# Head norm factor of 14 heads through memory instead of through TensorE

## The chip, the cores and the metric

One Trainium2 chip, one of its cores. The metric is the device time of one execution in microseconds (us). TensorE (PE in the profile) multiplies matrices, VectorE (DVE), ScalarE (ACT) and GpSimd (POOL) do the work on elements, SyncE (SP) issues DMAs, and 16 DMA engines move the data. Each engine runs its instructions in the order in which they are written and waits on semaphores for the others.

## The reference

A trunk of two layers over 512 positions of width 1024, in float32. Each layer is a half-step SwiGLU, a mixer and a second half-step SwiGLU. The mixer projects the normed input to q, k, v, an output gate, a convolution's input and two gates, runs a gated delta rule over 8 heads of width 128 and a depthwise convolution of 31 taps, and mixes the two. The part that matters here is the norm of each head's output:

```
def rmsnorm(x, w):
    xf = x.astype(jnp.float32)
    y = xf * lax.rsqrt(jnp.mean(xf * xf, axis=-1, keepdims=True) + EPS)
    return (y * w.astype(jnp.float32)).astype(x.dtype)

    o = gated_delta_chunked(q, k, v, g, beta)
    o = rmsnorm(o, head_norm) * jax.nn.silu(g_out.reshape(shp).astype(jnp.float32))
    y_a = o.reshape(bsz, seq, KEY_WIDTH).astype(h.dtype) @ w_a_out
```

The head's output stands with its 128 channels in the partitions and the 512 positions along the free axis. The factor (the power -0.5 of the mean square) is one number for each position, so it has to be the same in all partitions before it can be multiplied on.

## The kernel before

Every large product is done in float32r in three passes: a weight tile is split into a rounded part w_hi (ScalarE) and a rest w_lo, the activations likewise, and TensorE adds hi*hi, hi*lo and lo*hi (function three). In the head stage the rest of the weights is made by ScalarE writing -w_hi into w_lo and GpSimd adding the raw weights to it by an accumulating DMA (function lo on GpSimd). SP loads the raw tiles into four slots.

For each layer the heads run as a pipeline. While TensorE runs the delta rule of head rn it also runs the projections of head rn+1, six tiles t = 0 to 5 of 12 pieces each. The list PE_ORDER sets how they alternate: H is one such piece, two 512-column matmuls; the other names are steps of the delta rule. The delta rule inverts a triangular matrix by doubling in six levels lv = 0 to 5, each of which is xt{lv}, y{lv} and xy{lv} on TensorE. ScalarE makes the pieces XO{lv}, XE{lv} of X for xt{lv} and y{lv}. VectorE makes YD (L1623) out of y{lv}'s result, and xy{lv} waits for YD and XT. Behind each YD VectorE does what the tuple behind[lv] says: "t" is a tap of the long convolution (about one 512-column instruction, cacc), (0, j), (1, j), (2, j) are taps of the short convolutions of q, k and v, "oF", "ohi", "olo" belong to the tail.

The tail of head rn-1 (the norm of its output) runs within head rn. ScalarE squares the output, GpSimd adds a term ("sum"), TensorE sums over the partitions by four matmuls with a column of ones ("so"), VectorE adds a constant (vE), GpSimd takes the power -0.5 ("rs", function mean_root, L1896), which leaves 128 x 4 numbers in sm. TensorE then turns the four columns, each spread over 128 columns, into bank 5 ("fb", L725), VectorE multiplies (oF, L1715) and splits the product into o_hi and o_lo (L1718, L1721), which TensorE reads only after the last head. The tail of head 7 of each layer runs after the heads with the same steps.

GpSimd's order in a head is: sum, the product for qd, rs, the second power rk, then the accumulating DMAs of the tiles c0+3, c0+4, ..., c0+8, each as soon as ScalarE has written the negative (L861). hf0 is the buffer hf[0]: ScalarE copies the convolution's value tile there (valb, L1012) at t = 4, and VectorE reads it as craw (L1567) in level 0 of the next head.

Of the kernel before, what the change touches and what calls it, by code (L numbers as in the profile page):

```python
# [17 lines left out]
P = 128  # L18
# [69 lines left out]
PE_ORDER = "H H gr kt H kk kq H so H H H x2t vt H H H xt0 y0 H H fb xy0".split()  # L88
# [8 lines left out]
PE_STEPS = [x for x in PE_ORDER if x not in ("H", "so", "fb")]  # L97
PE_TAIL = ["so", "fb"]
# [18 lines left out]
def trunk(nc, x, params_in, ffn1_w_gate, ffn1_w_up, ffn1_w_down, w_in, w_ab, a_log, dt_bias, head_norm, w_a_out, w_b_out, w_o,  # L117
          ffn2_w_gate, ffn2_w_up, ffn2_w_down, consts, out):
    ds = bass.ds
    with ExitStack() as ctx:  # L120
# [63 lines left out]
        valb, gth, sgn, sgc, og = hf[0], hf[1], sqb[0], sqb[1], ssq  # L184
        S, R, VN = (sb(n, [P]) for n in ("S", "R", "VN"))
# [33 lines left out]

        def sem(name):  # L220
            return ctx.enter_context(nc.semaphore(name))
# [24 lines left out]
        ghi_done = sem("ghi_done")  # L246
        mrinv_done = sem("mrinv_done")
# [188 lines left out]
        def _(pe):  # L436
# [138 lines left out]
            for l in range(DEPTH):  # L575
# [139 lines left out]
                def tail(name, rn):  # L715

                    if name == "so":
                        pe.wait_ge(po_tl.sem, po_tl.after(rn, "sum"))
                        pe.wait_ge(ve_tl.sem, ve_tl.after(rn - 1, "oF"))
                        for c in range(NC):  # L720
                            m = mm(bank[5][:, c:c + 1], attn[:, c * P:c * P + P], ones[:, 0:1])
                    else:
                        pe.wait_ge(po_tl.sem, po_tl.after(rn, "rs"))
                        for c in range(NC):
                            m = nc.tensor.transpose(bank[5][:, c * P:c * P + P], whole(sm[:, 5, c:c + 1]), ident)  # L725
                    m.then_inc(*pe_tl.step(name))

# [64 lines left out]
                for m_ in range(PRE):  # L792
                    c = 2 * PRE + m_
                    first_unit(c)
                    for k in range(KT - 1):
# [10 lines left out]
                        if m_ == 1 and k == 4:  # L806
                            tail("fb", last)
# [42 lines left out]
        def _(act):  # L850
# [112 lines left out]
            for l in range(DEPTH):  # L963
# [17 lines left out]
                def dense_steps(t, Rd, c0, rd):  # L981
# [28 lines left out]
                    elif t == 4:  # L1010
                        act.wait_ge(ve_cr.sem, ve_cr.after(rd - 1, "craw"))
                        nc.scalar.activation(valb[:, :], bk[:, :], ACT.Copy).then_inc(*ac_ds.step("val"))  # L1012
# [216 lines left out]
        def _(dve):  # L1229
# [164 lines left out]
            for l in range(DEPTH):  # L1394
# [124 lines left out]
                def head(dense, hn, rn, before=True):  # L1519
# [75 lines left out]
                    behind = [("l", "a", "l", "c"), ("oF", "t", "ohi", "t", "olo", "t"), ((0, 0), "t", (0, 1), "t", (0, 2)),  # L1595
                              ("t", "t", "t", "t", "t"), ((1, 0), "t", (1, 1), "t", (1, 2)),
# [108 lines left out]
                def tail(name, rn, hn=None):  # L1705
# [7 lines left out]
                    elif name == "oF":  # L1713
                        dve.wait_ge(pe_tl.sem, pe_tl.after(rn, "fb"))
# [247 lines left out]
```

## Time and profile before

| | us |
|---|---|
| median of 3 runs | 2720.67 |
| lowest and highest | 2720.61, 2720.92 |
| the profiled execution | 2720.52 |
| its span, first to last instruction | 2718.7 |

Mean granted TensorE clock 0.999. Busy shares of the span: TensorE 100%, VectorE 58%, ScalarE 40%, GpSimd 9%. The time of an execution holds 1.8 us around the span. In a timeline row the first number is the start and the second the duration; matmuls and also neighbouring instructions of one engine overlap by a little, so the distance between starts, not the duration, is what one costs. A bracket at the end says how long the engine was idle before it and what ended that. Where rows of several kinds of matmul are merged, line 438 is the helper through which most of them are issued.

### The profile page before, as it was taken

Reading aid. Unit: us, or ns where it says so; the run is one execution under the profiler, and the core shown is the slowest. Engines: PE = TensorE matmul, PEld = TensorE weight load, DVE = VectorE, ACT = ScalarE, POOL = GpSimd, SP = SyncE. Lnnn points to the kernel's source line nnn. Section 1 sums busy time; section 2 is a strip of 40 time slices with the busy share of each in tenths; the row PEclk is TensorE's granted clock in tenths of the full one; section 3 lists DMA queues with packets and bytes.
Section 4 is the critical chain, followed back from the end, with each engine's and each line's share of the span. In section 5 each row is a group of like instructions: output and inputs, shape, how many; then the busy total and the mean of one; then the engine's idle time right before and its main releaser. Section 6 shows DMA issues by size and latency. Waiting matters only on the chain.

```text
span 2718.7 us, 35832 instructions
## 1 busy us (share of the span) xinstructions
PE 2705.3 (100%) x13096; PEld 2251.9 (83%) x13096; DVE 1581.7 (58%) x2504; ACT 1100.1 (40%) x1849; POOL 258.2 (9%) x231
## 2 busy tenths in 40 slices
PE   9999999999999999999999999999999999999998
PEld 7888878888887888888888888788888878888887
DVE  6554357888885345553355543688888943455532
ACT  4222247766663232222222222566676622322222
POOL 0000022122120010000000000211212100100000
PEclk9999999999999999999999999999999999999999
DMA  4223335554542222233322233455556332222332
GB/s 166 96 97 104 92 101 140 130 142 111 136 126 93 98 88 100 93 101 93 102 93 93 100 93 96 108 131 140 125 124 145 96 108 93 93 100 93 97 94 66
DMA packets 84603, 292.04 MB, mean 107 GB/s; under 512 B 10001, under 2 KB 12689, under 8 KB 84497
## 3 DMA queue, kind: packets, MB, share of 16 engines
q1 hardware_dynamic: 69232, 235.85, 26.5%
q0 software_dynamic: 14976, 54.53, 10.9%
q8 instruction: 64, 1.05, 0.2%
q14 instruction: 43, 0.34, 0.0%
q10 hardware_dynamic: 288, 0.27, 0.0%
HBM read 233.99 MB, written 2.10 MB: 87 GB/s over the span
## 4 chain that ended last, share of the span: by engine, by line
PE 97%; DVE 2%; ACT 0%; issue 0%; DMA 0%; DVEq 0%; POOLq 0%; POOL 0%; ACTq 0%
PE bank L438 95%; PE bank L637 1%; PE bank L689 1%; DVE c_lo L1747 0%; DVE w_lo L1235 0%; ACT c_hi L1191 0%; PE bank L651 0%; PE bank L725 0%; DVE sqb L1743 0%; DVE hf L1743 0%; DMA pcol<-in_params_in 0%; DVE hf L1738 0%; PE bank L458 0%; DVE NT L1664 0%; ACT w_hi L855 0%
## 5 line engine op out<-in xcount | busy, mean ns | idle before, releaser
L1235 DVE TENSOR_TENSOR w_lo<-raw,w_hi 128x1024 fp32r<-128x1024 f32 x342 | 422.6, 1237 | 542.2 <-ACT w_hi L855 542.1
L855 ACT ACTIVATE w_hi<-raw 128x1024 fp32r<-128x1024 f32 x446 | 469.8, 1055 | 658.7 <-PE bank L438 658.6
L438 PE MATMUL bank<-h_hi,w_hi 128*128 128x512 f32 x1504 | 587.1, 390 | 2.2 <-DVE h_lo L1260 2.1
L438 PE MATMUL bank<-h_hi,w_lo 128*128 128x512 f32 x1504 | 585.5, 389 | 0.0
L438 PE MATMUL bank<-h_lo,w_hi 128*128 128x512 f32 x1504 | 585.3, 389 | 0.0
L438 PE MATMUL bank<-g_hi,w_hi 128*128 128x512 f32 x928 | 384.2, 414 | 0.0
L438 PE MATMUL bank<-g_hi,w_lo 128*128 128x512 f32 x928 | 378.7, 408 | 0.0
L438 PE MATMUL bank<-g_lo,w_hi 128*128 128x512 f32 x928 | 369.6, 398 | 0.0
L438 PEld LDWEIGHTS bank<-h_hi,w_hi 128*128 128x128 f32 x1504 | 282.3, 188 | 63.3 <-issue 3.6
L438 PEld LDWEIGHTS bank<-h_hi,w_lo 128*128 128x128 f32 x1504 | 282.3, 188 | 58.8
L1535 DVE SCALAR_TENSOR_TENSOR cacc<-c_raw,ncol,cacc 128x512 f32<-128x512 f32 x464 | 330.0, 744 | 0.4
L438 PEld LDWEIGHTS bank<-h_lo,w_hi 128*128 128x128 f32 x1504 | 282.4, 188 | 57.7
L438 PE MATMUL bank<-act_hi,w_hi 128*128 128x512 f32 (+1 forms) x726 | 281.3, 387 | 0.0
L438 PE MATMUL bank<-act_hi,w_lo 128*128 128x512 f32 (+1 forms) x726 | 279.6, 385 | 0.0
L438 PE MATMUL bank<-act_lo,w_hi 128*128 128x512 f32 (+1 forms) x726 | 277.0, 382 | 0.0
L890 ACT ACTIVATE hf<-hf 128x512 f32<-128x512 f32 x88 | 55.6, 632 | 447.3 <-DVE hf L1282 447.3
L1845 POOL TENSOR_TENSOR ssq<-ssq,sqb 128x512 f32<-128x512 f32 x41 | 54.8, 1337 | 1708.0 <-ACT sqb L869 1708.0
L438 PEld LDWEIGHTS bank<-g_hi,w_lo 128*128 128x128 f32 x928 | 175.0, 189 | 31.3
L438 PEld LDWEIGHTS bank<-g_lo,w_hi 128*128 128x128 f32 x928 | 175.5, 189 | 28.2
L438 PEld LDWEIGHTS bank<-g_hi,w_hi 128*128 128x128 f32 x928 | 175.9, 190 | 22.9
L438 PEld LDWEIGHTS bank<-act_hi,w_lo 128*128 128x128 f32 x726 | 136.2, 188 | 30.0
L438 PEld LDWEIGHTS bank<-act_lo,w_hi 128*128 128x128 f32 x726 | 136.3, 188 | 28.7
(258 smaller groups left out, 3355.5 us busy)
## 6 DMA issues: line engine op xcount, KB each, us to landing
raw<-in_w_in SPq DMA_DIRECT2D x128, 512.0 KB, 3.3
w_lo<-raw POOLq DMA_DIRECT2D x104, 512.0 KB, 4.6
raw<-in_ffn_w_gate SPq DMA_DIRECT2D x88, 512.0 KB, 3.2
raw<-in_ffn_w_up SPq DMA_DIRECT2D x88, 512.0 KB, 3.2
raw<-in_ffn_w_down SPq DMA_DIRECT2D x64, 512.0 KB, 3.5
raw<-in_ffn_w_down SPq DMA_DIRECT2D x32, 384.0 KB, 3.1
raw<-in_w_a_out SPq DMA_DIRECT2D x16, 512.0 KB, 3.2
raw<-in_w_b_out SPq DMA_DIRECT2D x16, 512.0 KB, 3.2
```

The source lines that it names most:

```text
L438: return nc.tensor.matmul(o, a, b, start=start, stop=stop, **kw)
L637: m = nc.tensor.transpose(o[:, c * P:c * P + P], a[:, c * P:c * P + P], ident)
L689: m = nc.tensor.transpose(bank[2][:, q * P:q * P + P], X[:, q * P:q * P + P], ident)
L855: nc.scalar.activation(w_hi[c % SLOTS][:, :], raw[c % SLOTS][:, :], ACT.Copy).then_inc(hi_done, 1)
L890: nc.scalar.activation(sg_f[f][:, :], sg_f[f][:, :], ACT.Silu).then_inc(silu_done, 1)
L1235: tt(w_lo[c % SLOTS][:, :], raw[c % SLOTS][:, :], w_hi[c % SLOTS][:, :].bitcast(F32), ALU.subtract).then_inc(lo_v, 1)
L1535: stt(out=acc[:, :], in0=src, scalar=ncol[:, j:j + 1], in1=acc[:, :], op0=ALU.mult, op1=ALU.add).then_inc(taps, 1)
L1845: tt(ssq[:, :], ssq[:, :], sqb[m % 2][:, :], ALU.add).then_inc(sums, 1)
```

## The change

For the heads 0 to 6 of each layer (14 in all) the factor no longer goes through TensorE. GpSimd, right after the power, writes the 128 x 4 numbers to a scratch in memory (rs_rows, one row of 512 for each head, 4-byte pieces), and later in the same head, behind the weight DMA of tile c0+4, reads that row into all 128 partitions (factor_row), into hf[0], between its use as craw and its next use as valb. VectorE's oF, ohi and olo stand behind YD of level 3 instead of level 1 and the five taps of level 3 stand in level 1; oF waits for the row and multiplies by it out of SBUF. ScalarE's valb waits for the oF of two heads before. In PE_ORDER "fb" is gone and xt0 y0 stand one H earlier. The last head's tail keeps its four columns (last_factor_spread).

```
--- before.py
+++ after.py
@@ -85,7 +85,7 @@
 
 
 
-PE_ORDER = "H H gr kt H kk kq H so H H H x2t vt H H H xt0 y0 H H fb xy0".split()
+PE_ORDER = "H H gr kt H kk kq H so H H H x2t vt H H xt0 y0 H H H xy0".split()
 for _l in range(1, LEVELS):
     PE_ORDER += ("H H H " if _l < LEVELS - 1 else "H H H H ").split() + f"xt{_l} y{_l} H H H xy{_l}".split()
 PE_ORDER += "H H H xtf H H H vn0 H H os0".split()
@@ -94,8 +94,8 @@
 HALVES = 12
 LATE = 8
 assert PE_ORDER.count("H") == 6 * HALVES, PE_ORDER.count("H")
-PE_STEPS = [x for x in PE_ORDER if x not in ("H", "so", "fb")]
-PE_TAIL = ["so", "fb"]
+PE_STEPS = [x for x in PE_ORDER if x not in ("H", "so")]
+PE_TAIL = ["so"]
 
 DVE_STEPS = ["hs", "kT", "qT", "dmin", "skE", "rden", "bnk2", "neg", "NT", "x2T", "vT", "yd0", "attnT"]
 DVE_STEPS += [f"yd{_l}" for _l in range(1, LEVELS)]
@@ -182,6 +182,7 @@
             sb(n, [SEQ]) for n in "qT kT dec thv attn qd NT X XT Y".split())
 
         valb, gth, sgn, sgc, og = hf[0], hf[1], sqb[0], sqb[1], ssq
+        row = hf[0]
         S, R, VN = (sb(n, [P]) for n in ("S", "R", "VN"))
         hsc = sb("hsc", [HEADS, HS_N, NC])
         hs = sb("hs", [HS_N, NC])
@@ -216,6 +217,8 @@
         csum, csq = hf[1], (hf[0], sqb[0])
 
         bank = [ctx.enter_context(nc.psum_tensor(f"bank{i}", [P, SEQ], F32)) for i in range(8)]
+
+        rs_rows = nc.dram_tensor("rs_rows", (DEPTH * HEADS, SEQ), F32, kind="Internal").ap()
 
         def sem(name):
             return ctx.enter_context(nc.semaphore(name))
@@ -244,6 +247,9 @@
         hf_done = sem("hf_done")
         hhi_done = sem("hhi_done")
         ghi_done = sem("ghi_done")
+        fb_done = sem("fb_done")
+        rs_out = sem("rs_out")
+        row_in = sem("row_in")
         mrinv_done = sem("mrinv_done")
         scaled = sem("scaled")
         hlo_g = sem("hlo_g")
@@ -714,16 +720,19 @@
 
                 def tail(name, rn):
 
-                    if name == "so":
-                        pe.wait_ge(po_tl.sem, po_tl.after(rn, "sum"))
+                    pe.wait_ge(po_tl.sem, po_tl.after(rn, "sum"))
+                    if rn == l * 8 and l:
                         pe.wait_ge(ve_tl.sem, ve_tl.after(rn - 1, "oF"))
-                        for c in range(NC):
-                            m = mm(bank[5][:, c:c + 1], attn[:, c * P:c * P + P], ones[:, 0:1])
-                    else:
-                        pe.wait_ge(po_tl.sem, po_tl.after(rn, "rs"))
-                        for c in range(NC):
-                            m = nc.tensor.transpose(bank[5][:, c * P:c * P + P], whole(sm[:, 5, c:c + 1]), ident)
+                    for c in range(NC):
+                        m = mm(bank[5][:, c:c + 1], attn[:, c * P:c * P + P], ones[:, 0:1])
                     m.then_inc(*pe_tl.step(name))
+
+                def last_factor_spread(rn):
+
+                    pe.wait_ge(po_tl.sem, po_tl.after(rn, "rs"))
+                    for c in range(NC):
+                        m = nc.tensor.transpose(bank[5][:, c * P:c * P + P], whole(sm[:, 5, c:c + 1]), ident)
+                    m.then_inc(fb_done, 1)
 
                 def xy(lv, rn):
                     pe.wait_ge(ac_dn.sem, ac_dn.after(rn, f"XT{lv}"))
@@ -804,7 +813,7 @@
                             pe.wait_ge(var_done, l * 4 + 3)
                             tail("so", last)
                         if m_ == 1 and k == 4:
-                            tail("fb", last)
+                            last_factor_spread(last)
                         three(m_, c % SLOTS, k, o_hi, o_lo, k, k == 0, False)
                 for m_ in range(PRE):
                     if m_ == 0:
@@ -1009,6 +1018,8 @@
                         nc.scalar.activation(gth[:, :], bk[:, :], ACT.Tanh, scale=0.5).then_inc(*ac_ds.step("g_th"))
                     elif t == 4:
                         act.wait_ge(ve_cr.sem, ve_cr.after(rd - 1, "craw"))
+                        if rd >= l * 8 + 2:
+                            act.wait_ge(ve_tl.sem, ve_tl.after(rd - 2, "oF"))
                         nc.scalar.activation(valb[:, :], bk[:, :], ACT.Copy).then_inc(*ac_ds.step("val"))
                     else:
                         act.wait_ge(ve_sg.sem, ve_sg.after(rd, "sg"))
@@ -1019,6 +1030,8 @@
                     act.wait_ge(taps, l * (8 * CONV) + (m + 2) * CONV)
                     if m >= 3:
                         act.wait_ge(csq_done, l * 7 + (m - 2))
+                    elif m == 2:
+                        act.wait_ge(ve_tl.sem, ve_tl.after(l * 8 + 6, "oF"))
                     dst = csum if m == 0 else csq[m % 2]
                     nc.scalar.activation(dst[:, :], c_all[:, m, :], ACT.Square).then_inc(cf_done, 1)
 
@@ -1592,8 +1605,8 @@
                             return
                         gate_product(dense[0])
 
-                    behind = [("l", "a", "l", "c"), ("oF", "t", "ohi", "t", "olo", "t"), ((0, 0), "t", (0, 1), "t", (0, 2)),
-                              ("t", "t", "t", "t", "t"), ((1, 0), "t", (1, 1), "t", (1, 2)),
+                    behind = [("l", "a", "l", "c"), ("t", "t", "t", "t", "t"), ((0, 0), "t", (0, 1), "t", (0, 2)),
+                              ("oF", "t", "ohi", "t", "olo", "t"), ((1, 0), "t", (1, 1), "t", (1, 2)),
                               ("t", "t", (2, 0), "t", (2, 1), "t", (2, 2))]
 
                     def put(items):
@@ -1711,8 +1724,12 @@
                         dve.wait_ge(pe_tl.sem, pe_tl.after(rn, "so"))
                         a = ts(sm[:, 4, :], bank[5][:, 0:NC], P * EPS * EPS, None, ALU.add)
                     elif name == "oF":
-                        dve.wait_ge(pe_tl.sem, pe_tl.after(rn, "fb"))
-                        a = tt(og[:, :], og[:, :], bank[5][:, :], ALU.mult)
+                        if rn == l * 8 + 7:
+                            dve.wait_ge(fb_done, l + 1)
+                            a = tt(og[:, :], og[:, :], bank[5][:, :], ALU.mult)
+                        else:
+                            dve.wait_ge(row_in, (rn + 1 - l) * 16)
+                            a = tt(og[:, :], og[:, :], row[:, :], ALU.mult)
                     elif name == "ohi":
                         dve.wait_ge(ve_tl.sem, ve_tl.after(rn, "oF"))
                         a = ts(o_hi[:, hn, :], og[:, :], 1.0, None, ALU.mult)
@@ -1883,6 +1900,15 @@
                             h_rest(l, 4 * t)
                             h_rest(l, 4 * t + 2)
                         lo(Rd, G, c0 + t + 4)
+                        if t == 0 and rn is not None and before:
+                            factor_row(rn - 1)
+
+                def factor_row(rn):
+
+                    pool.wait_ge(rs_out, (rn + 1 - l) * 16)
+                    pool.wait_ge(ve_cr.sem, ve_cr.after(rn + 1, "craw"))
+                    src = rs_rows[rn].rearrange("(o s) -> o s", o=1)
+                    pool.dma_start(out=row[:, :], in_=src.broadcast_to([P, SEQ])).then_inc(row_in, 16)
 
                 def square_sum(rn):
 
@@ -1894,6 +1920,9 @@
 
                     pool.wait_ge(ve_tl.sem, ve_tl.after(rn, "vE"))
                     tt(sm[:, 5, :], sm[:, 4, :], pw[:, 0, :], ALU.pow).then_inc(*po_tl.step("rs"))
+                    if rn != l * 8 + 7:
+                        pool.wait_ge(po_tl.sem, po_tl.after(rn, "rs"))
+                        pool.dma_start(out=rs_rows[rn].rearrange("(c i) -> i c", c=NC), in_=sm[:, 5, :], allow_slow_non_contiguous=True).then_inc(rs_out, 16)
 
                 Gh = l * G_LAYER - 1
                 head(Rh, Gh, 0, None)
```

On VectorE, the piece of one head from the YD of level 3 to the YD of level 4. Before:

```order
L1623 TENSOR_TENSOR YD<-bank,cst 128x256
L1535 SCALAR_TENSOR_TENSOR cacc_95<-c_raw,ncol,cacc_95 128x512
L1535 SCALAR_TENSOR_TENSOR cacc_94<-c_raw,ncol,cacc_94 128x512
L1535 SCALAR_TENSOR_TENSOR cacc_95<-c_raw,ncol,cacc_95 128x512
L1535 SCALAR_TENSOR_TENSOR cacc_94<-c_raw,ncol,cacc_94 128x512
L1535 SCALAR_TENSOR_TENSOR cacc_95<-c_raw,ncol,cacc_95 128x512
L1623 TENSOR_TENSOR YD<-bank,cst 128x256
```

Now:

```order
L1636 TENSOR_TENSOR YD<-bank,cst 128x256
L1732 TENSOR_TENSOR ssq<-ssq,hf_74 128x512
L1548 SCALAR_TENSOR_TENSOR cacc_95<-c_raw,ncol,cacc_95 128x512
L1735 TENSOR_SCALAR o_hi<-ssq 128x512
L1548 SCALAR_TENSOR_TENSOR cacc_94<-c_raw,ncol,cacc_94 128x512
L1738 TENSOR_TENSOR o_lo<-ssq,o_hi 128x512
L1548 SCALAR_TENSOR_TENSOR cacc_95<-c_raw,ncol,cacc_95 128x512
L1636 TENSOR_TENSOR YD<-bank,cst 128x256
```

Lines 1732, 1735 and 1738 are oF, ohi and olo; hf_74 is hf[0], the row. They stood behind the YD of level 1 with three taps between them, and stand now behind the YD of level 3, with all that VectorE does later behind them.

On GpSimd, one head from the product for qd to the weights of tile c0+5. Before:

```order
L1876 TENSOR_TENSOR qd<-qd,qT 128x512
L1896 TENSOR_TENSOR sm<-sm,pw 128x4
L1879 TENSOR_TENSOR sm<-sm,pw 128x4
L1837 DMA w_lo_65<-raw_57 128x1024
L1837 DMA w_lo_62<-raw_54 128x1024
L1837 DMA w_lo_63<-raw_55 128x1024
```

Now:

```order
L1893 TENSOR_TENSOR qd<-qd,qT 128x512
L1922 TENSOR_TENSOR sm<-sm,pw 128x4
L1925 DMA rs_rows<-sm 128x4x1
L1896 TENSOR_TENSOR sm<-sm,pw 128x4
L1854 DMA w_lo_65<-raw_57 128x1024
L1854 DMA w_lo_62<-raw_54 128x1024
L1911 DMA hf_74<-rs_rows 128x512
L1854 DMA w_lo_63<-raw_55 128x1024
```

Two DMAs have come in: the write to the scratch ahead of the second power, and the read of the row between the weights of c0+4 and those of c0+5.

On TensorE, level 0 of one head from the turned X of level 0 to xy0. Before:

```order
L438 MATMUL bank<-g_lo,w_hi_58 128x512
L689 MATMUL bank<-cst,X 128x128 x2
L438 MATMUL bank<-X,Y 128x128 x2
L438 MATMUL bank<-g_hi,w_lo_62 128x512
L438 MATMUL bank<-g_hi,w_hi_58 128x512
L438 MATMUL bank<-g_lo,w_hi_58 128x512
L438 MATMUL bank<-g_hi,w_lo_62 128x512
L725 MATMUL bank<-cst,sm 128x128 x4
L438 MATMUL bank<-YD,XT 128x64x2 x2
```

Now (one row earlier, the last piece ahead of level 0 is not the same one):

```order
L444 MATMUL bank<-g_hi,w_lo_62 128x512
L695 MATMUL bank<-cst,X 128x128 x2
L444 MATMUL bank<-X,Y 128x128 x2
L444 MATMUL bank<-g_hi,w_hi_58 128x512
L444 MATMUL bank<-g_lo,w_hi_58 128x512
L444 MATMUL bank<-g_hi,w_lo_62 128x512
L444 MATMUL bank<-g_hi,w_hi_58 128x512
L444 MATMUL bank<-g_lo,w_hi_58 128x512
L444 MATMUL bank<-g_hi,w_lo_62 128x512
L444 MATMUL bank<-YD,XT 128x64x2 x2
```

L725 was the four turned columns, and the matmuls of X (L689, now L695) with those of X,Y are xt0 and y0. The columns are gone and one H, two rows of g, has moved from ahead of xt0 to behind y0.

## Rows read from the trace of the kernel before

**Rows 1.** The page: busy time by engine; the chain that ended last, by engine.

```profile
PE 2705.3 (100%) x13096; PEld 2251.9 (83%) x13096; DVE 1581.7 (58%) x2504; ACT 1100.1 (40%) x1849; POOL 258.2 (9%) x231
...
PE 97%; DVE 2%; ACT 0%; issue 0%; DMA 0%; DVEq 0%; POOLq 0%; POOL 0%; ACTq 0%
```

**Rows 2.** TensorE's waits: line, releaser, us in total, times, longest.

```profile
PE bank L438 <- DVE h_lo L1260: 2.1, 2, 1.9
```

**Rows 3.** Timeline of TensorE in one head: start us, us, instruction.

```profile
518.90 0.38 PE L689 MATMUL bank<-cst,X 128*128 128x128 f32 x2
...
520.49 0.60 PE L725 MATMUL bank<-cst,sm 128*128 128x128 f32 x4
520.92 0.61 PE L438 MATMUL bank<-YD,XT 128*128 128x128 f32 x4
521.29 0.48 PE L438 MATMUL bank<-g_hi,w_hi 128*128 128x512 f32 x1
```

**Rows 4.** The instructions of line 725: count, ns, first and last start.

```profile
L725 PE MATMUL bank<-cst,sm x64: 270/272/273, 471.4 to 2164.1; 128*128 128x128 f32 x64
```

**Rows 5.** Timeline of GpSimd in the same head.

```profile
517.66 1.52 POOL L1879 TENSOR_TENSOR sm<-sm,pw 128x4 f32<-128x4 f32 x1
519.47 0.92 POOL L1837 DMA_DIRECT2D w_lo<-raw  x1 [0.28 <-issue]
530.23 0.86 POOL L1837 DMA_DIRECT2D w_lo<-raw  x1 [9.85 <-ACT w_lo L861]
```

**Rows 6.** Timeline of ScalarE in the same head.

```profile
517.55 0.38 ACT L1079 ACTIVATE X<-bank 128x256 f32<-128x256 f32 x1
...
528.61 1.05 ACT L861 ACTIVATE w_lo<-raw 128x1024 fp32r<-128x1024 f32 x1
...
544.73 1.05 ACT L855 ACTIVATE w_hi<-raw 128x1024 fp32r<-128x1024 f32 x1
```

**Rows 7.** DMA from 530 to 535 us: busy tenths in 40 slices; issue and landing.

```profile
DMA  0000000000000986919919199097891990100000
...
w_lo<-raw POOLq DMA_DIRECT2D x1, 512.0 KB, 4.5
```

**Rows 8.** Timeline of VectorE in the same head.

```profile
523.97 0.68 DVE L1715 TENSOR_TENSOR ssq<-ssq,bank 128x512 f32<-128x512 f32 x1
524.56 0.54 DVE L1530 TENSOR_SCALAR cacc<-c_raw,ncol 128x512 f32<-128x512 f32 x1
...
525.35 0.48 DVE L1532 TENSOR_SCALAR cacc<-c_raw,ncol 128x512 f32<-128x512 f32 x1
...
526.35 0.75 DVE L1535 SCALAR_TENSOR_TENSOR cacc<-c_raw,ncol,cacc 128x512 f32<-128x512 f32 x1
...
531.41 0.42 DVE L1623 TENSOR_TENSOR YD<-bank,cst 128x256 f32<-128x256 f32 x1 [0.16 <-PE bank L438]
531.75 3.39 DVE L1535 SCALAR_TENSOR_TENSOR cacc<-c_raw,ncol,cacc 128x512 f32<-128x512 f32 x5
535.30 0.42 DVE L1623 TENSOR_TENSOR YD<-bank,cst 128x256 f32<-128x256 f32 x1 [0.16 <-PE bank L438]
...
538.30 0.74 DVE L1434 SCALAR_TENSOR_TENSOR ka<-k_raw,dcol,ka 128x512 f32<-128x512 f32 x1
```

**Rows 9.** Timeline of TensorE in the same head, later.

```profile
536.50 0.61 PE L438 MATMUL bank<-YD,XT 128*128 128x128 f32 x4
...
540.84 0.61 PE L438 MATMUL bank<-YD,XT 128*128 128x128 f32 x4
```

**Rows 10.** DMA at the end of the run: GB/s in 40 slices.

```profile
GB/s 344 353 297 315 372 344 344 344 358 334 353 348 226 5 0 0 0 0 0 0 0 80 358 339 301 358 358 334 344 320 372 353 330 348 367 245 14 0 0 0
```

**Rows 11.** DMA from 371 to 376 us: issues, KB each, us to landing.

```profile
wab_raw<-in_w_ab SPq DMA_DIRECT2D x1, 64.0 KB, 1.7
alb<-in_a_log SPq DMA_DIRECT2D x1, 4.0 KB, 2.8
```

**Rows 12.** Window at the end: busy by engine, granted clock, DMA share, GB/s.

```profile
2712.00:2718.00 6.00, 0.43 (x2) 0.19 (x2) 2.41 (x3) 0.00 (x0) 0.24 (x1) 0.68 0.65 218
```

More of the change, by code:

```diff
@@ L82, in after @@
         return (rnd + 1) * len(self.names) + self.at[name]
-PE_ORDER = "H H gr kt H kk kq H so H H H x2t vt H H H xt0 y0 H H fb xy0".split()
+PE_ORDER = "H H gr kt H kk kq H so H H H x2t vt H H xt0 y0 H H H xy0".split()
 for _l in range(1, LEVELS):
@@ L96 @@
 assert PE_ORDER.count("H") == 6 * HALVES, PE_ORDER.count("H")
-PE_STEPS = [x for x in PE_ORDER if x not in ("H", "so", "fb")]
-PE_TAIL = ["so", "fb"]
+PE_STEPS = [x for x in PE_ORDER if x not in ("H", "so")]
+PE_TAIL = ["so"]
 DVE_STEPS = ["hs", "kT", "qT", "dmin", "skE", "rden", "bnk2", "neg", "NT", "x2T", "vT", "yd0", "attnT"]
@@ L184, in trunk @@
         valb, gth, sgn, sgc, og = hf[0], hf[1], sqb[0], sqb[1], ssq
+        row = hf[0]
         S, R, VN = (sb(n, [P]) for n in ("S", "R", "VN"))
@@ L246, in trunk @@
         ghi_done = sem("ghi_done")
+        fb_done = sem("fb_done")
+        rs_out = sem("rs_out")
+        row_in = sem("row_in")
         mrinv_done = sem("mrinv_done")
@@ L715, in tail, with last_factor_spread @@
                 def tail(name, rn):
-                    if name == "so":
-                        pe.wait_ge(po_tl.sem, po_tl.after(rn, "sum"))
+                    pe.wait_ge(po_tl.sem, po_tl.after(rn, "sum"))
+                    if rn == l * 8 and l:
                         pe.wait_ge(ve_tl.sem, ve_tl.after(rn - 1, "oF"))
[L720 to L725, printed above, removed]
-                    m.then_inc(*pe_tl.step(name))
+                    for c in range(NC):
+                        m = mm(bank[5][:, c:c + 1], attn[:, c * P:c * P + P], ones[:, 0:1])
+                    m.then_inc(*pe_tl.step(name))
+                def last_factor_spread(rn):
+                    pe.wait_ge(po_tl.sem, po_tl.after(rn, "rs"))
+                    for c in range(NC):
+                        m = nc.tensor.transpose(bank[5][:, c * P:c * P + P], whole(sm[:, 5, c:c + 1]), ident)
+                    m.then_inc(fb_done, 1)
                 def xy(lv, rn):
@@ L1885, in head, with factor_row @@
                         lo(Rd, G, c0 + t + 4)
+                        if t == 0 and rn is not None and before:
+                            factor_row(rn - 1)
+                def factor_row(rn):
+                    pool.wait_ge(rs_out, (rn + 1 - l) * 16)
+                    pool.wait_ge(ve_cr.sem, ve_cr.after(rn + 1, "craw"))
+                    src = rs_rows[rn].rearrange("(o s) -> o s", o=1)
+                    pool.dma_start(out=row[:, :], in_=src.broadcast_to([P, SEQ])).then_inc(row_in, 16)
                 def square_sum(rn):
```

22 lines of the change are left out of this document (17 added, 5 removed).

## The prediction

> **What bounds the kernel now.** I read first the page: TensorE is busy in 2705.3 of 2718.7 us, and 97% of the chain that ended last is TensorE's own work [rows 1]. Then the waits of TensorE: the longest sum for one releaser is 2.1 us in the whole run [rows 2]. So TensorE never waits in the head stage. An instruction taken off it is worth its full time, and every microsecond for which a semaphore holds it is lost at once, as it runs in written order with nothing idle to take up the delay. What matters is therefore not VectorE's or GpSimd's busy share but how near each of their results comes to the TensorE instruction that wants it. For that I took the timelines of one head of layer 0 (the one whose four turned columns start at 520.49) and laid the engines beside each other. Heads follow each other every 49.12 us (the same columns start at 471.4 in the head before, the first start of [rows 4]), so one stands for the 14.
>
> **What is removed.** Four transposes of a column, L725, 64 in all [rows 4]: 16 groups, of which 14 go and the two of the last head of each layer stay. From the start of the group to the start of the next one, 520.49 to 520.92, it takes 0.43 us [rows 3], not the 0.60 shown as its duration, since matmuls overlap. 14 x 0.43 = 6.0 us saved. The place of xt0 and y0 moves forward by one H (two matmuls, some 0.47 us), so that three H stand between y0 and xy0 in place of two and the four columns. xt0 was at 518.90 and comes to 518.43; ScalarE's XE0, the later of the two pieces it needs, is over at 517.93 [rows 3, 6], so this makes no wait. Within the head everything TensorE does after them is then 0.43 us earlier, and ScalarE, which follows it, too.
>
> **What is added.** (1) GpSimd sends the 512 factors to memory, as 4-byte pieces. The pow that makes them is over when the next one starts, at 517.66, and GpSimd's next issue is at 519.47 [rows 5]. Its weight DMA keeps GpSimd 0.86 us for 128 pieces; four times the pieces cost between 0.86 and 3.4 us. Then the weight DMA of 519.47 starts at 520.4 to 523 and GpSimd is free by 524. After 519.47 it does nothing until 530.23, so I price this at nothing. SP's load into that slot waits for the weights' landing and comes as much later; ScalarE copies the slot next at 544.73 [rows 6], over ten microseconds on. Without that cover (beyond some 9 us) the DMA at 530.23 would be late.
> (2) GpSimd reads the row into 128 partitions, behind the weight DMA of 530.23 in its own order. That one waits for ScalarE's negative copy, 528.61 to 529.66 [rows 6]; 0.43 us earlier it starts at 529.80 and leaves GpSimd at 530.66. With the 0.28 us that GpSimd needs between its instructions [rows 5] the row's DMA starts at 530.94. Behind it is the next weight DMA, over five us later, so GpSimd itself has room.
> (3) VectorE's multiplication oF, ohi and olo move from level 1 to level 3, and oF waits for the row to land. Level 3 begins for VectorE with YD at 531.41 [rows 8], now 530.98, so VectorE asks for the row at 531.32: less than half a microsecond after its DMA is issued. That oF reads the row from SBUF and not from PSUM I price at nothing (one tensor_tensor of the same size, 0.68 us). ScalarE writes the row's buffer again as valb, behind its copy of 544.73, and waits there for an oF that is long over by then. Behind oF on VectorE are the rest of level 3 and then the YD of level 4, and for that YD waits TensorE's xy4 (the group at 536.50 [rows 9]).
>
> **When the row lands.** The trace shows no DMA queued right behind another of GpSimd's. It shows the one ahead of it alone: issued at 530.23, data in the slices from 531.6 to 534.4 on all engines, landed after 4.5 us [rows 7], some 0.4 us behind its last data. In the new run its data end 0.43 us earlier, at 533.9. The row's packets go to the same 16 engines from the same queue, so I let them start then. 0.26 MB at the 350 GB/s of a busy stretch [rows 10] take 0.75 us. Against that, the 4 KB of a_log read into 128 partitions took 2.8 us from issue, and 64 KB without repetition 1.7 [rows 11]: reading one place 128 times costs up to 1.1 us more, 1.85 in all. I take 1.1 us, nearer to the plain rate as the sum of bytes is large. Landing: 533.9 + 1.1 + 0.4 = 535.4; bounds with queueing 535.0 and 536.2.
> On the order of the packets the Trainium skill (DMA: Bandwidth & Descriptors, section Queues, rings and completion order) says that an engine works through the descriptors of one queue in the order in which they were put there. No row here shows it; by it the row stands behind the weights, as I take it.
>
> **From the row to TensorE.** oF and its companions with three taps between them: level 1 of before did it from 523.97 to 527.10 where the first two taps are short (0.54 and 0.48 us) [rows 8]. Level 3 has full taps of 0.74 us, so 3.13 + 0.20 + 0.26 = 3.59, less 0.08 us by which neighbours overlap (five taps of 0.74 take 3.39): 3.51 us to YD. YD 0.42 us, and 0.05 us each for the two semaphores, assumed: 4.03 us. xy4 can start at 535.4 + 4.03 = 539.43. Without a wait it would stand at 536.50 - 0.43 = 536.07. TensorE waits 3.36 us in each head.
> Is more lost behind it? Level 4 gives VectorE 3.74 us of work from YD to YD (535.30 to 539.04), so the next YD starts at 542.7 and ends at 543.1; xy5 stands 4.34 us behind xy4 [rows 9], at 543.8. No second wait. Nor is anything regained: all of TensorE's work behind xy4 waits with it.
> Sum: 14 x 3.36 = 47.0, less 6.0 = +41.0 us. The profiled execution took 2720.5 us (span 2718.7), within 0.2 us of the median shown, 2720.7. 2720.5 + 41.0 = 2761.5 us.
>
> **Rivals.**
> *The row is not held by the weights ahead of it* (15%). Landing then by GpSimd's own delay: issue at 530.94, 1.4 us to the first data [rows 7], 0.75 for the data and 0.4 to the landing: 533.5. xy4 at 537.53, a wait of 1.46, and 14 x (1.46 - 0.43) = 14.4: 2735 us. For it: slices with 1 or 0 stand between the full ones in [rows 7]. Against: the weight packets still have to be moved by the same engines.
> The Trainium skill (DMA: Bandwidth & Descriptors, section Anatomy of one DMA) prices a DMA of GpSimd at 2.0 us and its bytes at 436 GB/s: an estimate of 2.6 us for this one, which is the time of this rival. For the weights it gives 3.2 us where the trace has 4.5, so it is low for the DMA that decides here.
> *Reading one row 128 times is slow* (15%). The 1.1 us of a_log may come once for each 512 bytes, so four times here: landing at 533.9 + 4.4 + 0.4 = 538.7, xy4 at 542.73, a wait of 6.66, 14 x (6.66 - 0.43) = 87: 2808 us, and anything between 2775 and this. Only the two small rows of [rows 11] speak for it.
> *TensorE loses its clock in the wait* (7%). Its mean granted clock over the run is 0.999 (the full one, 2.4 GHz); it falls only after TensorE's last work, and the mean in 2712 to 2718 is 0.68 [rows 12]. A wait of 3.4 us is longer than any of before. If the 3.9 us of a level then ran at 1.2 GHz, twice as long, up to 14 x 3.9 = 55 us would come on top: 2816 us.
> *No wait at all, faster* (4%). The removed 6.0 us remain where the row lands by 532.0 (536.07 - 4.03): 2714.5 us. That is 1.1 us from its issue. The quickest DMA of these rows took 1.7 us and GpSimd's own 4.5. It decides only if the factor row's DMA gets ahead of the weight DMA, or the records of issue are late by more than a microsecond. A landing near 532.5 would make no difference that can be told (1%).
> *The row isn't what oF waits for*: were the write of the factors slow (over 9 us), its landing would hold the read and all of GpSimd's weights. That is a longer wait in the same place, and is in the upper part of the range.
>
> **How the numbers follow.** The forecast, a landing between 534.9 and 536.2, has 58% and alone gives 2755 to 2773. The range goes down to the unqueued row (2732), and up into the slow row's cases, to 2790: left out are 5% below and about half of the slow row and the clock's case above. What this measurement can tell from no change is 0.2%, 5.4 us. Slower by more than that: all cases but two, 0.94; within it 0.02; faster 0.04.
>
> **What would show it.** In the profile after: L725's successor has 8 instructions in place of 64. TensorE gets a row of waits, on its matmuls, for VectorE's YD, 14 times and 3.4 us each, about 47 us in all. VectorE is idle before the oF line for some 4 us each, put down to the row's DMA. The row's DMA has a time to landing near 4.5 us (2.6 with the rival). The heads come 52 us apart instead of 49.1. The prediction is wrong if oF does not wait (landing within a microsecond), if the DMA lands before the weights' ahead of it, or if the granted clock falls in the stage.

## The result, and the profile of the changed kernel

The changed kernel takes 2797.70 us (median of 4 runs, 2796.44 to 2798.78), the kernel before 2720.73 (4 runs, 2720.61 to 2720.92): ratio 1.0282, 95% interval 1.0268 to 1.0297. That is 77 us slower where 41 were forecast, and above the range, which ended at 2790. In the profiled executions the span went from 2718.7 to 2797.0 us: +78.3.

The page of after, busy time by engine and the chain by engine, against [rows 1]:

```profile
PE 2726.0 (97%) x13040; PEld 2263.9 (81%) x13040; DVE 1581.5 (57%) x2504; ACT 1101.9 (39%) x1849; POOL 272.5 (10%) x259
...
PE 89%; DVE 4%; DMA 3%; ACT 2%; issue 1%; POOL 0%; DVEq 0%; POOLq 0%; ACTq 0%
```

TensorE has 56 matmuls fewer and is busy 20.7 us longer. The chain, which was nearly all TensorE's own work, now runs in part through DMA and VectorE. The mean granted clock is 0.989, where it was 0.999. The two things to explain are thus a wait, and work that takes longer.

TensorE's waits in after, against [rows 2], and below them the first of VectorE's that is new:

```profile
PE bank L444 <- DVE YD L1636: 58.5, 14, 4.9
```

```profile
DVE ssq L1732 <- DMA hf<-rs_rows: 69.2, 14, 5.6
```

This is the wait forecast, at the place forecast, 14 times: oF (L1732) waits for the row, YD (L1636) stands behind oF, and xy4 behind YD. But it is 4.18 us a head, not 3.36. One head shows both parts. TensorE from the last matmul ahead of xy4 on, against [rows 9]:

```profile
543.28 0.39 PE L444 MATMUL bank<-g_lo,w_hi 128*128 128x512 f32 x1
543.51 0.39 PE L444 MATMUL bank<-g_hi,w_lo 128*128 128x512 f32 x1
548.78 1.20 PE L444 MATMUL bank<-YD,XT 128*128 128x128 f32 x4 [4.88 <-DVE YD L1636]
...
550.20 0.63 PE L444 MATMUL bank<-g_lo,w_hi 128*128 128x512 f32 x1
550.63 0.63 PE L444 MATMUL bank<-g_hi,w_lo 128*128 128x512 f32 x1
```

A 512-column matmul is 0.23 us from start to start ahead of the wait and 0.43 behind it. The windows of after show the granted clock (the column behind the engines'):

```profile
543.00:546.00 3.00, 0.90 (x4) 0.38 (x3) 1.32 (x3) 1.46 (x5) 0.87 (x1) 0.99 0.45 128
546.00:548.00 2.00, 0.00 (x0) 0.00 (x0) 2.00 (x5) 0.00 (x0) 0.00 (x0) 0.50 0.91 242
548.00:552.00 4.00, 3.22 (x10) 2.77 (x11) 3.94 (x7) 0.66 (x2) 0.00 (x0) 0.50 0.53 105
552.00:556.00 4.00, 4.00 (x23) 3.37 (x22) 2.15 (x4) 2.60 (x5) 0.00 (x0) 0.91 0.38 128
```

0.50 is the lower level, 1.2 GHz. It came within the wait of 4.88 us, at 545.9, when TensorE had stood still for 2.0 us; in other heads it came up to 1.2 us behind the wait's end. The clock fell in 12 of the 14 heads: 58.0 us at half clock in the head stages, in 47.6 of which TensorE worked. That work takes twice as long, so half of it is lost, 23.8 us.

Why the row is late is in the same head. GpSimd and, below, the DMAs issued there (KB, us to landing), against [rows 5, 7]:

```profile
525.65 0.85 POOL L1925 DMA_DIRECT2D rs_rows<-sm  x1 [0.30 <-POOL sm L1922]
526.52 1.05 POOL L1896 TENSOR_TENSOR sm<-sm,pw 128x4 f32<-128x4 f32 x1
527.51 0.95 POOL L1854 DMA_DIRECT2D w_lo<-raw  x1
537.48 0.86 POOL L1854 DMA_DIRECT2D w_lo<-raw  x1 [9.01 <-ACT w_lo L870]
538.02 0.90 POOL L1911 DMA_DIRECT2D hf<-rs_rows  x1
```

```profile
rs_rows<-sm POOLq DMA_DIRECT2D x1, 2.0 KB, 9.1
...
w_lo<-raw POOLq DMA_DIRECT2D x1, 512.0 KB, 9.7
...
w_lo<-raw POOLq DMA_DIRECT2D x1, 512.0 KB, 6.6
hf<-rs_rows POOLq DMA_DIRECT2D x1, 256.0 KB, 6.6
```

The write of the factors lands after 9.1 us. The weights of c0+3 behind it land after 9.7, at 537.2; SP, which waits for that to load the slot again, does so only then:

```profile
537.34 7.20 SPq L365 DMA_DIRECT2D raw<-in_w_in  x2
```

(Two loads merged: the first goes out at 537.34, the second at 544.21.) The first is in flight until 541.24, together with the weights of c0+4, issued at 537.48. These land after 6.6 us, and the row behind them after 6.6. VectorE, against [rows 8]:

```profile
538.65 0.42 DVE L1636 TENSOR_TENSOR YD<-bank,cst 128x256 f32<-128x256 f32 x1 [0.16 <-PE bank L444]
544.68 0.69 DVE L1732 TENSOR_TENSOR ssq<-ssq,hf 128x512 f32<-128x512 f32 x1 [5.61 <-DMA hf<-rs_rows]
...
548.22 0.42 DVE L1636 TENSOR_TENSOR YD<-bank,cst 128x256 f32<-128x256 f32 x1
```

oF starts at 544.68 and xy4 at 548.78: 4.10 us, forecast 4.03. The rest of the late time is the DMA's.

### The profile page after: what moved, and what is told of

It reads as the page before. It is cut to its first block, busy times and chain, and to the rows that moved or that the text cites. A ratio compares the mean times of both kernels' runs of the same rounds, so it can differ in the third digit from the quotient of the medians.

```text
span 2797.0 us, 35751 instructions
## 1 busy us (share of the span) xinstructions
PE 2726.0 (97%) x13040; PEld 2263.9 (81%) x13040; DVE 1581.5 (57%) x2504; ACT 1101.9 (39%) x1849; POOL 272.5 (10%) x259
## 4 chain that ended last, share of the span: by engine, by line
PE 89%; DVE 4%; DMA 3%; ACT 2%; issue 1%; POOL 0%; DVEq 0%; POOLq 0%; ACTq 0%
PE bank L444 88%; DMA hf<-rs_rows 3%; DVE cacc L1548 1%; PE bank L643 1%; PE bank L695 1%; ACT w_hi L864 1%; ACT w_lo L870 1%; DVE w_lo L1248 0%; DVE o_lo L1738 0%; DVE c_lo L1764 0%; DVE ssq L1732 0%; ACT c_hi L1204 0%; POOL w_lo L1854 0%; PE bank L657 0%; ACT dec L1101 0%
## 5 line engine op out<-in xcount | busy, mean ns | idle before, releaser
L444 PE MATMUL bank<-g_hi,w_hi 128*128 128x512 f32 x928 | 392.9, 423 | 0.0
L444 PE MATMUL bank<-g_lo,w_hi 128*128 128x512 f32 x928 | 375.9, 405 | 0.0
```

The source lines that it names most:

```text
L444: return nc.tensor.matmul(o, a, b, start=start, stop=stop, **kw)
```

## The experiments

Each is the changed kernel with one edit, unless it says otherwise. A DMA "lands" when its data have arrived and those who wait for it may go on. The theory: the wait and the clock together make the 78 us, and the slow write makes the wait longer than forecast. The rivals: the row's own read is slow, or TensorE's slower work has another cause than its idleness.

| kernel | us (median, range) | ratio to before, 95% | TensorE waits for YD |
|---|---|---|---|
| row first | 2720.49 (2718.42 to 2721.82) | 0.9999 (0.9989 to 1.0008) | 3.3 |
| 16-byte write | 2799.97 (2795.01 to 2801.13) | 1.0287 (1.0270 to 1.0304) | 54.0 |
| level 5 | 2719.27 (2718.89 to 2720.03) | 0.9995 (0.9985 to 1.0005) | none |
| busy wait | 2772.71 (2771.39 to 2776.61) | 1.0189 (1.0172 to 1.0206) | 8.1 |
| row first, level 4 | 2714.98 (2714.53 to 2715.27) | 0.9979 (0.9970 to 0.9988) | none |
| ScalarE's queue | 2718.75 (2716.80 to 2719.83) | 0.9991 (0.9982 to 1.0001) | 1.4 |
| before with the write | 2720.73 (2720.24 to 2721.02) | 1.0000 (0.9991 to 1.0010) | none |
| half busy | 2779.16 (2777.78 to 2780.47) | 1.0216 (1.0201 to 1.0232) | 28.8 |
| ScalarE's queue, late | 2740.30 (2738.97 to 2741.68) | 1.0074 (1.0057 to 1.0090) | 16.5 |
| 16-byte write, plain read | 2787.77 (2785.78 to 2788.73) | 1.0248 (1.0231 to 1.0265) | 48.6 |

**Is it the weights ahead of the row?** The row's DMA goes ahead of the weights of c0+4:

```
-                        lo(Rd, G, c0 + t + 4)
                         if t == 0 and rn is not None and before:
                             factor_row(rn - 1)
+                        lo(Rd, G, c0 + t + 4)
```

> GpSimd issues the row's read ahead of the weight DMA of tile c0+4 instead of behind it; nothing else differs from the changed kernel. Theory (the row is late because its packets stand behind those weights in one queue): it is then issued when its own write has landed, some 2.5 us before the weights, has only the weights of c0+3 ahead of it and lands about 538.5 in the head where VectorE asks for it at 539.1. No wait of TensorE for YD, no fall of the clock, 2713 to 2718 us. Rival (the read of one row into 128 partitions takes 6 us wherever it stands): it lands at 540.8, TensorE still waits 1.1 us a head and the time is near 2730 us. If the weights of c0+4 were now late instead, TensorE would wait on them.

The wait fell from 58.5 to 3.3 us, in 6 heads, the clock did not fall, and the time came back to that of before. It is not the 2713 to 2718 expected: the row, now issued as soon as the write has landed, still took 4.6 to 6.3 us, and oF waited for it a little in each head (12.0 us in all). TensorE waited for no weights that it had not waited for before. This edit puts the row ahead of the weights and also issues it some 3 us earlier; which of the two helps is taken up again below. GpSimd in the same head of the version with this order and oF at level 4 (below), whose issues stand in the same order:

```profile
517.68 0.85 POOL L1925 DMA_DIRECT2D rs_rows<-sm  x1 [0.30 <-POOL sm L1922]
518.56 1.05 POOL L1896 TENSOR_TENSOR sm<-sm,pw 128x4 f32<-128x4 f32 x1
519.55 0.94 POOL L1854 DMA_DIRECT2D w_lo<-raw  x1
526.65 0.58 POOL L1911 DMA_DIRECT2D hf<-rs_rows  x1 [6.17 <-DMA rs_rows<-sm]
529.51 0.86 POOL L1854 DMA_DIRECT2D w_lo<-raw  x1 [2.27 <-ACT w_lo L870]
```

The 6.17 us for which the slow write holds GpSimd are free here: the next weights wait for ScalarE anyway.

**Is it the slow write?** 128 pieces of 16 bytes in place of 512 of 4, and VectorE's oF reads the row in steps of four:

```
-  pool.dma_start(out=rs_rows[rn].rearrange("(c i) -> i c", c=NC), in_=sm[:, 5, :], ...)
+  pool.dma_start(out=rs_rows[rn].rearrange("(i c) -> i c", c=NC), in_=sm[:, 5, :])
-  a = tt(og[:, :], og[:, :], row[:, :], ALU.mult)
+  a = tt(chunked(og), chunked(og), row[:, :].rearrange("p (i c) -> p c i", c=NC), ALU.mult)
```

> The scratch is written as 128 pieces of 16 bytes in the order in which they lie in SBUF, and VectorE's multiplication reads the row with a stride of four instead; the place of all instructions is that of the changed kernel. Theory (the 512 4-byte pieces keep the DMA engines busy, delay the weights of c0+3, by these SP's load, and by that the weights of c0+4): the write lands within 4 us instead of 8.9, the weights of c0+3 in under 6 instead of 7 to 10, those of c0+4 in 4.5 to 4.8 and the row in 4.5 to 5.2 instead of 5.2 to 6.6. TensorE waits 3.0 to 3.5 us a head, 45 us in all, and loses its clock in fewer heads: 2757 to 2775 us. Rival (small pieces cost nothing and the row itself is slow): 2798 us as before, all landings as they were.

The landings came near to the theory's, those of c0+4 later than its 4.5 to 4.8 us. The same two DMAs and the oF of one head:

```profile
w_lo<-raw POOLq DMA_DIRECT2D x1, 512.0 KB, 5.1
hf<-rs_rows POOLq DMA_DIRECT2D x1, 256.0 KB, 5.2
```

```profile
541.70 1.07 DVE L1732 TENSOR_TENSOR ssq<-ssq,hf 128x512 f32<-128x512 f32 x1 [4.15 <-DMA hf<-rs_rows]
```

The write landed after 1.8 us (at most 2.5), the weights behind it after 4.5 to 4.7 in most heads, and SP's load was over before c0+4 was issued. But the time did not move: oF took 1.07 us for 0.69, so the waits stayed at 3.6 to 3.9 us (one 4.6), and the clock fell in all 14 heads (59.0 us of work at half clock, 29.5 lost). Two things had changed at once here; the next version keeps the plain read, which puts the factors at the wrong positions (its output is not the reference's):

```
-  pool.dma_start(out=rs_rows[rn].rearrange("(c i) -> i c", c=NC), in_=sm[:, 5, :], ...)
+  pool.dma_start(out=rs_rows[rn].rearrange("(i c) -> i c", c=NC), in_=sm[:, 5, :])
```

> The changed kernel with the scratch written in 128 pieces of 16 bytes and read as it lies there, without the strided read of the multiplication; the factors then stand at the wrong positions of the row, so the output is not the reference's. Theory (the 4-byte pieces cost 0.7 us of wait a head through the delayed weights, and in the first run with 16-byte pieces the strided read gave 0.37 us of it back to the path): every head waits 3.4 us, 48 us in all, in place of 58; with the clock falling in some heads 2767 to 2785 us. Rival (the size of the pieces does not matter for the time): 2795 us or more.

2787.77 us, 3 above the 2785 at which the theory ended and 7 below the rival. TensorE's waits are now nearly equal, 3.2 to 3.5 us (one 4.24):

```profile
PE bank L444 <- DVE YD L1636: 48.6, 14, 4.2
```

3.47 a head: the forecast's 3.36, with a row that lands 5.2 us after its issue in 13 of 14 heads. So the 4-byte pieces cost 58.5 - 48.6 = 9.9 us of wait. The clock fell in 10 heads (38.1 us of work, 19.0 lost).

That the pieces act through SP's load is a reading of the times, and no run moves that load alone; but the changed kernel's own heads bear it out. Where the load was still in flight for less than 2 us behind the issue of c0+4 (3 heads), the row landed after 5.2 to 5.3 us; where it was for 2.3 to 4.0 us (11 heads), after 5.9 to 6.6, but for one with 5.3. Why the write itself takes so long stays open: the trace has 16 records of 128 bytes for it in either version, in the second head of 0.12 to 0.20 us each with the 4-byte pieces and of 0.03 with the others, and no record of the time from there to the landing.

**Does the write cost anything where nothing tight stands behind it?** The kernel before, with the write alone:

```
+  pool.wait_ge(po_tl.sem, po_tl.after(rn, "rs"))
+  pool.dma_start(out=rs_rows[rn].rearrange("(c i) -> i c", c=NC), in_=sm[:, 5, :], ...)
```

> The kernel before, with the write of the factors to the scratch in 4-byte pieces added on GpSimd for the 14 heads; nothing reads it, the four columns stay on TensorE. Theory (the write is hidden as long as nothing tight stands behind it): the weights of c0+3 land 7 to 10 us after their issue instead of 4.6, those of c0+4 in up to 6, and the time stays 2720.7 us. Rival (the delayed weights cost TensorE time by themselves): 2723 us or more, with waits for the weights.

It does not, at a landing of 8.0 to 8.9 us and weights behind it after 6.7 to 9.2 (4.5 to 6.1 in before). The write's landing:

```profile
DMA to landing us min/median/max: 8.0/8.4/8.9
```

**Is the slower work due to idleness?** 32 transposes of no use stand before xy4, so that TensorE has work for 3.62 us of the wait:

```
+  elif name == "xy4" and before:
+      for _ in range(32):
+          nc.tensor.transpose(bank[5][:, 256:256 + P], ident, ident)
+      run_stage(name, rn)
```

> TensorE runs 32 transposes of no use (3.4 us of work) into free columns of bank 5 right before xy4 of every head that waits; else the changed kernel. The output is the same. Theory (26 of the 77 us are a clock that falls to 1.2 GHz because TensorE stands still for some 4 us): the wait shrinks to what is left of 4.2 us, the clock stays up, and the kernel with more work is faster: 2768 to 2778 us. Rival (the wait alone, or the DMA traffic, makes matmuls slow, or the clock falls anyway): 2798 us or more, since in the five heads with waits of 3.4 to 3.5 us nothing is left to hide in.

TensorE in one head of it:

```profile
595.99 0.40 PE L444 MATMUL bank<-g_hi,w_lo 128*128 128x512 f32 x1
596.23 3.66 PE L778 MATMUL bank<-cst 128*128 128x128 f32 x32
599.85 0.68 PE L444 MATMUL bank<-YD,XT 128*128 128x128 f32 x4
600.29 0.48 PE L444 MATMUL bank<-g_hi,w_hi 128*128 128x512 f32 x1
600.61 0.39 PE L444 MATMUL bank<-g_lo,w_hi 128*128 128x512 f32 x1
```

xy4 comes no earlier (oF still waits for the row), but behind it the matmuls are 0.23 us apart and the clock fell in one head only: 448 matmuls more, and 25 us faster than the changed kernel. Transposes (14 x 3.62 = 50.7 us) and what is left of the waits (8.1) make 58.8 us, as long as the waits alone were (58.5), so what is saved is the clock. With 16 of them (1.81 us):

> As the run with 32 useless transposes ahead of xy4, but with 16 (1.7 us), so that TensorE stands still for 1.7 to 3.2 us instead of 3.4 to 4.9. Theory (what costs is how long it stands still, and the clock fell in every head that waited 3.6 us or more and in part of those that waited 3.4 to 3.6): the clock falls in a few heads at most, 2771 to 2782 us. Rival (any wait of over a microsecond drops the clock): it falls in most heads, 2790 us or more.

```profile
PE bank L444 <- DVE YD L1640: 28.8, 14, 2.5
```

2779.16 us. Behind waits of 1.46 to 2.51 us the clock fell in 4 heads, the shortest of their waits being 1.88 us; in 3 heads with waits of 2.34 to 2.51 us it did not. So neither every wait of over a microsecond drops it, as the rival had it, nor does it take one of over 3 us.

**Does a later user help by itself?** oF, ohi and olo go behind YD of level 5, oF with one tap ahead of it:

```
-  ("oF", "t", "ohi", "t", "olo", "t"), ((1, 0), "t", (1, 1), "t", (1, 2)),
-  ("t", "t", (2, 0), "t", (2, 1), "t", (2, 2))]
+  ("t", "t", "t", "t", "t"), ((1, 0), "t", (1, 1), "t", (1, 2)),
+  ("t", "oF", (2, 0), "ohi", (2, 1), "t", "olo", (2, 2))]
```

> VectorE's oF, ohi and olo stand behind the YD of level 5 with one tap ahead, instead of level 3, whose place taps take; both DMAs are as in the changed kernel. Theory (all of the loss comes from TensorE's wait behind oF): the row has landed over 2 us before it is asked for, no wait, no fall of the clock, 2713 to 2718 us. Rival (the DMAs themselves, by their traffic or by the weights that they delay, cost a part): what they cost stays, 2725 us or more.

2719.27 us, 1.3 above the theory's 2718 and below the rival's 2725. With the slow write and the weights ahead of the row left in, no wait for YD is left. The heads are 48.69 us apart, 0.43 less than in before: the saving of the columns, as forecast. Of the saving 3.6 us are lost again at the end of the stages:

```profile
PE bank L643 <- ACT X L1161: 3.6, 2, 1.8
```

There ScalarE's square for the convolution (m = 2) waits for the last oF, 1.8 us in each layer, and with it the work that TensorE wants. The move to level 4 with the row first avoids both:

```
-  ("oF", "t", "ohi", "t", "olo", "t"), ((1, 0), "t", (1, 1), "t", (1, 2)),
+  ("t", "t", "t", "t", "t"), ("oF", (1, 0), "ohi", (1, 1), "olo", (1, 2)),
```

> Both moves together and one level only: GpSimd issues the row's read ahead of the weights of c0+4, and VectorE's oF, ohi and olo stand behind the YD of level 4 (taps take their place in level 3). In the run with the read ahead the row landed 0 to 2 us too late for level 3, in the run with oF in level 5 the last head of each layer lost 1.8 us because ScalarE's square for the convolution waits for that oF. Theory: neither is left, every head is 0.43 us shorter than before, 2714.5 us (2713.5 to 2716), a ratio near 0.998. Rival (the two DMAs cost something that no wait shows): 2718 us or more.

2714.98 us in 11 runs, 5.8 below before and the fastest of all: ratio 0.9979 (0.9970 to 0.9988). VectorE in it:

```profile
534.58 0.42 DVE L1636 TENSOR_TENSOR YD<-bank,cst 128x256 f32<-128x256 f32 x1 [0.16 <-PE bank L444]
534.92 0.68 DVE L1732 TENSOR_TENSOR ssq<-ssq,hf 128x512 f32<-128x512 f32 x1
...
538.94 0.42 DVE L1636 TENSOR_TENSOR YD<-bank,cst 128x256 f32<-128x256 f32 x1 [0.41 <-PE bank L444]
```

oF no longer waits; the row had landed 2.6 us before (2.6 to 4.0 over the heads), and VectorE even waits 0.41 us for TensorE at the next YD.

**Is it the queue, or the DMA engines?** The row's DMA is issued by ScalarE, behind its negative copy of c0+4 in written order:

```
+  act.wait_ge(rs_out, (rn - l) * 16)
+  act.wait_ge(ve_cr.sem, ve_cr.after(rn, "craw"))
+  act.dma_start(out=row[:, :], in_=src.broadcast_to([P, SEQ])).then_inc(row_in, 16)
```

> The row is read by a DMA of ScalarE's queue, issued behind its negative copy for c0+4, at the time at which GpSimd issues those weights; all else as in the changed kernel. Theory (in the changed kernel the row waits for the weights' packets ahead of it in GpSimd's own queue): from its own queue it lands within 2.5 to 4 us of its issue, before the weights, TensorE waits 0 to 1 us a head and keeps its clock: 2715 to 2730 us. Rival (the 16 DMA engines are what is taken, or the read of one row by all partitions is slow in itself): it lands with the weights, 5 us or more after its issue, TensorE waits over 3 us a head: 2760 us or more.

It did not test that, since the DMA went out earlier than written (ScalarE's rows of one head):

```profile
575.67 0.38 ACT L1097 ACTIVATE XT<-bank 128x256 f32<-128x256 f32 x1 [0.95 <-PE bank L695]
575.85 0.35 ACTq L1144 DMA_DIRECT2D hf<-rs_rows  x1
575.95 0.41 ACT L1101 ACTIVATE dec<-NT 128x256 f32<-128x256 f32 x1
576.26 1.05 ACT L864 ACTIVATE w_hi<-raw 128x1024 fp32r<-128x1024 f32 x1
577.21 1.04 ACT L870 ACTIVATE w_lo<-raw 128x1024 fp32r<-128x1024 f32 x1
```

The negative copy at 577.21 stands ahead of the DMA in the program; the DMA, at 575.85, waited for the landing of the write alone (issued at 567.00, landed at 575.30). So it acted as "row first" did, also in the row's landing: 4.0 to 6.1 us, median 5.4, where "row first" had 4.6 to 6.3, median 5.4. No weights stand ahead of it in ScalarE's queue, but SP's load of 512 KB goes out at about the same time (575.94 in this head). That fits engines shared between the queues better than an order within one. The next one makes ScalarE wait for its own copy first:

```
+  act.wait_ge(neg_done, ... * 4 + c0 + 5)
```

> As the run with the row's read on ScalarE's queue, which went out 3 us early there, as soon as the write had landed, ahead of the two activations written before it. Here ScalarE first waits for its own negative copy of c0+4, so that the read starts when these weights are released too, half a microsecond ahead of GpSimd's weight DMA and one ahead of where the changed kernel had it. Theory (in the changed kernel the row stood behind the weights in GpSimd's queue): from a queue of its own it lands 3 to 4 us after its issue and ahead of the weights, TensorE waits under 0.7 us a head: 2715 to 2724 us. Rival (the engines are taken by the weights in whichever queue the row stands): it lands 5 us or more after its issue, TensorE waits 2 us or more a head: 2740 us or more.

```profile
583.40 0.33 ACTq L1145 DMA_DIRECT2D hf<-rs_rows  x1
```

Here GpSimd issues the weights of c0+4 at 583.96. The row landed after 3.6 to 5.0 us (median 4.2), ahead of those weights, and TensorE waited 16.5 us in all. So landing and wait lie between the theory (4 us, 0.7) and the rival (5 us, 2), while the time, 2740.30, is already the rival's 2740. The wait is 1.2 us a head in place of 4.2; about 1.1 us of that gain is the earlier issue, the rest the quicker landing ahead of the weights. But also from a queue of its own, with the weights issued 0.56 us behind it and SP's load in flight, the row takes 4.2 us, not the 2.6 of the prediction's unqueued rival; what it would take with nothing else in flight no run shows. The Trainium skill (DMA: Bandwidth & Descriptors, section Anatomy of one DMA) puts a DMA of GpSimd's of this size at an estimated 2.6 us; this one, from ScalarE, is longer by more than half.

**The sum.** The version of 2714.98 has the same work without the wait, so its profile (span 2712.9, TensorE busy 2700.2) is the zero for the others. Busy time added is split into the transposes of no use and half of the work done at half clock:

| kernel | span added | waits for YD | busy added | of it transposes | of it clock |
|---|---|---|---|---|---|
| changed | 84.1 | 58.5 | 25.8 | | 23.8 |
| 16-byte write | 85.0 | 54.0 | 30.4 | | 29.5 |
| same, plain read | 71.1 | 48.6 | 22.1 | | 19.0 |
| half busy | 63.1 | 28.8 | 34.0 | 25.3 | 6.6 |
| busy wait | 61.9 | 8.1 | 53.8 | 50.7 | 1.7 |
| ScalarE, late | 24.4 | 16.5 | 7.4 | | 1.7 |

Wait and busy time make up each span to within 0.6 us. The zero itself is 5.8 below before: the columns. What is left of the busy time, 1 to 3 us and 5.7 in the last row, stays open.

## Why the prediction was wrong

Forecast were +41.0 us, measured +77. The wait was found, at its place and for its reason; two prices in the sum failed. The write of the factors was priced at nothing and cost 9.9 us of wait, and the clock behind the wait had no term in the sum and cost 23.8 us.

*What is removed*: right. 0.43 us a head is what the heads lose in distance where nothing waits, and 5.8 us in all, forecast 6.0. That xt0 and y0 make no new wait was right too.

*What is added, step (1), "I price this at nothing"*: this step failed. The argument was that nothing follows until 530.23 and that the landing must stay under some 9 us. It looked at GpSimd's time, and the issue is as cheap as said (0.85 us). The landing is 8.6 to 9.9 us, and the weights behind it, SP's load behind those, and the weights of c0+4 beside that load are all later, down to the row. The prediction named that load as "over ten microseconds" from mattering for ScalarE; it mattered for the DMA engines. It is 9.9 us of the 58.5. That it is the write's pieces is shown by the 16-byte version with the plain read; that they are harmless where nothing tight stands behind them, by before with the write. The Trainium skill (DMA: Bandwidth & Descriptors, section Why small descriptors are slow (HBM only)) explains the loss on small pieces by about three bus cycles for each packet and 32 bytes of metadata for each DMA operation. The runs have 8.4 us for 2 KB in 512 pieces and 1.8 in 128; the section has no time for such a write to hold against this.

*When the row lands*: right in the main. The row always landed behind the weights ahead of it, by 0.6 us in this head. With the write's delay taken out it landed 5.2 us after its issue, 5.7 after the weights'; forecast 5.6. Two errors cancel in it: the row was issued 0.54 us after the weights, not 1.14, and its data took less than the 1.1 us assumed, but the weights themselves took 5.1 instead of 4.5 with the row behind them. That GpSimd's second DMA waits its turn was not separated from contention on the engines.

*From the row to TensorE*: right, 4.10 us for 4.03. *No second wait*: right.

*The sum*: this is the second step that failed, and the dearer one: the clock's fall stood as a rival with 7% and not in the sum. "TensorE loses its clock in the wait" was listed with the right mechanism, and its price of up to 3.9 us a head was too high: 47.6 us of work at half clock, 3.4 a head, lose half of that, 1.7. It should have been a term of the forecast: each wait forecast was 3.36 us, and behind waits of that length (the plain 16-byte version, 3.2 to 3.5 us) the clock fell in 9 of 13 heads. With it the sum would have been 41 + 19 = 60, and with the write's 10 and the 5 more that longer waits cost in clock, 75. The slow row (15%) did not occur: the row landed 0.6 to 0.8 us after the weights ahead of it. Nor did the unqueued row: even ahead of the weights no row landed within 3.6 us of its issue (2.6 in the rival). The range failed because both misses were on one side, and 2790 left room for one.

## What to carry to other kernels

Where a change makes the bound engine wait, ask at once what its clock does behind the wait: here waits of 3.2 to 4.9 us cost another 1.4 to 2.1 us a head on the average of a run, and a wait filled with useless matmuls was 25 us cheaper than an idle one. A DMA that feeds a tight consumer is priced by all that stands ahead of it in its queue and by what those landings release; a tiny write in 4-byte pieces at the front was worth 10 us at the end. The remedy was not in speeding anything up but in order: the row ahead of the weights and its user one level later turned +77 us into -5.8.

## What the runs showed of the hardware

- A write of 2 KB to memory in 4-byte pieces lands after 8.0 to 9.9 us and holds up the DMA behind it (512 KB after 6.7 to 9.2 us in place of 4.5 to 6.1, in before with and without the write); in 16-byte pieces it lands after 1.8 us in most heads.
- ScalarE's DMA goes out when its own semaphores allow, ahead of activations written before it: at 575.85, with two of them still to start at 576.26 and 577.21.
- TensorE's clock can fall behind waits as short as 1.88 us (with 1.81 us of transposes ahead) and 1.94 us (ScalarE's queue, late, with none), and stayed up behind waits of 3.44 and 3.54 (the changed kernel) and of 3.50 us (16-byte write, plain read): length alone does not decide it in these runs.
- VectorE's multiplication of 512 columns takes 1.07 us in place of 0.69 when one operand is read in steps of four.
- GpSimd's DMA of the row starts 0.54 us after that of the weights, in all 14 heads, though each is shown as 0.86 to 0.90 us long.
